# Weaving the high and low parts of three matmul operands in one SBUF tensor

## The reference

```python
# first block: four branches a, b, c, d, each of width 256
yi = y.reshape(B, S, BRANCH_W) * jax.nn.silu(z)
term = jax.nn.sigmoid(h @ w_merge[i]) * (yi @ w_br[i])
# second block, each of two layers
o = jnp.einsum('bhsm,bmhd->bshd', p.astype(v.dtype), v).reshape(B, S, D_MODEL)
x = x + o @ w_o                                        # memory output
x = x + (jax.nn.silu(h @ w_gate) * (h @ w_up)) @ w_down  # down projection
```

## Time and profile before

| | |
|---|---|
| median of 3 runs | 1111.04 us (1110.3 to 1111.07) |
| the profiled execution, span | 1111.3 us (no other time of it is recorded) |
| TensorE matmuls | 1092.0 us busy, 98%, 6251 instructions |
| TensorE weight loads | 951.6 us busy, 86%, 6251 instructions |
| VectorE | 749.5 us, 67% |
| ScalarE | 583.6 us, 53% |
| GpSimd | 54.4 us, 5% |
| HBM | 193 MB read, 175 GB/s over the span |

### The profile page before, as it was taken

The page is one execution under the profiler, slowest core; times in us unless marked ns, Lnnn a source line. Parts: engine busy times, 40 slices in busy tenths (PEclk is TensorE's granted clock), DMA queues, the critical chain, the costliest instruction groups (busy, mean ns, idle before and its releaser), DMA issues.

```text
span 1111.3 us, 15418 instructions
## 1 busy us (share of the span) xinstructions
PE 1092.0 (98%) x6251; PEld 951.6 (86%) x6251; DVE 749.5 (67%) x1024; ACT 583.6 (53%) x940; POOL 54.4 (5%) x87
## 2 busy tenths in 40 slices
PE   8999999999999999999999999999999999999997
PEld 6799988788898988989988988788988989888986
DVE  5736776865679977555678855546967546788643
ACT  3458653444477775555444544456765545444442
POOL 3311000000010000001000000000011000000000
PEclk9999999999999999999999999999999999999999
DMA  9956464655654325535555555544445435555550
GB/s 343 381 161 207 135 196 162 233 184 189 223 168 126 115 77 189 175 99 149 197 184 184 196 182 196 189 153 151 152 153 189 132 115 190 190 190 189 162 179 38
DMA packets 118776, 195.09 MB, mean 176 GB/s; under 512 B 6586, under 2 KB 39762, under 8 KB 118705
## 3 DMA queue, kind: packets, MB, share of 16 engines
q1 hardware_dynamic: 116144, 187.51, 50.7%
q0 software_dynamic: 2560, 6.60, 2.0%
HBM read 193.04 MB, written 1.05 MB: 175 GB/s over the span
## 4 chain that ended last, share of the span: by engine, by line
PE 83%; DVE 10%; ACT 5%; issue 1%; DMA 1%; POOL 1%; SPq 0%; DVEq 0%; ACTq 0%; POOLq 0%
PE product L669 55%; PE small L706 5%; PE product L706 5%; DVE conv_out L2719 5%; PE product L708 3%; PE small L708 3%; PE product L996 3%; ACT w_high L591 1%; ACT diagonal L2612 1%; DVE w_low L601 1%; PE small L816 1%; PE small L2081 1%; PE small L731 1%; PE small L1462 1%; PE small L1451 1%
## 5 line engine op out<-in xcount | busy, mean ns | idle before, releaser
L601 DVE TENSOR_TENSOR w_low<-w_raw,w_high 128x2048 fp32r<-128x2048 f32 (+3 forms) x160 | 350.0, 2190 | 180.2 <-ACT w_high L591 178.6
L591 ACT ACTIVATE w_high<-w_raw 128x2048 fp32r<-128x2048 f32 (+3 forms) x160 | 292.1, 1832 | 175.9 <-PE product L669 144.2
L669 PE MATMUL product<-w_high,H 128*128 128x512 f32 (+2 forms) x736 | 239.7, 393 | 0.5 <-DVE w_low L601 0.5
L669 PEld LDWEIGHTS product<-w_high,H 128*128 128x128 f32 x736 | 137.9, 188 | 26.9 <-DVE w_low L601 0.9
L669 PE MATMUL product<-H,w_high 128*128 128x256 f32 x816 | 150.9, 283 | 0.1
L669 PE MATMUL product<-w_low,H 128*128 128x512 f32 (+2 forms) x368 | 142.3, 387 | 0.0
L669 PEld LDWEIGHTS product<-H,w_high 128*128 128x128 f32 x816 | 126.6, 188 | 1.1 <-DVE w_low L601 0.5
L669 PE MATMUL product<-H,w_low 128*128 128x256 f32 x408 | 114.2, 280 | 0.0
L706 PE MATMUL product<-H,w_high 128*128 128x512 f32 x256 | 89.1, 391 | 0.0
L706 PE MATMUL small<-H,w_high 128*128 128x512 f32 x256 | 89.1, 391 | 0.0
L669 PEld LDWEIGHTS product<-w_low,H 128*128 128x128 f32 x368 | 69.3, 188 | 11.9 <-issue 0.2
(11 more groups left out here) (412 smaller groups left out, 1784.3 us busy)
## 6 DMA issues: line engine op xcount, KB each, us to landing
w_raw<-in_ffn_w_gate SPq DMA_DIRECT2D x20, 1024.0 KB, 5.0
w_raw<-in_ffn_w_up SPq DMA_DIRECT2D x20, 1024.0 KB, 5.0
w_raw<-in_ffn_w_down SPq DMA_DIRECT2D x20, 1024.0 KB, 5.0
w_raw<-in_w_merge SPq DMA_DIRECT2D x16, 1024.0 KB, 5.2
w_raw<-in_w_ada SPq DMA_DIRECT2D x32, 256.0 KB, 6.5
w_raw<-in_mem_w_k SPq DMA_DIRECT2D x8, 1024.0 KB, 5.0
w_raw<-in_mem_w_v SPq DMA_DIRECT2D x8, 1024.0 KB, 5.0
w_raw<-in_conv_w_pw SPq DMA_DIRECT2D x16, 512.0 KB, 4.7
```

The source lines that it names most:

```text
L591: k.act.eng.activation(parts_of(k, i, j)[0], raw_of(k, i), ACT.Copy).then_inc(*k.act.tells("weights_high", ("weights high", i)))
L601: k.vec.eng.tensor_tensor(low, raw, high.bitcast(F32), ALU.subtract).then_inc(*k.vec.tells("weights_low", ("weights low", i)))
L669: mm = pe.eng.matmul(bank[:, off:off + wide], a, r, start=b not in started, stop=True, skip_group_check=True)
```

## The change

A new method makes one tensor in which each element is followed by its partner: high, low, high, low. The two views step two elements, 8 bytes. Three operands get it in place of the pair. Sizes, the places of all other tensors, the instructions, their order and their waits stay the same.

```diff
+    def woven(self, name, tiles, n=S):
+
+        both = self.sb(name, [P, tiles, n, 2], F32R)
+        return both[:, :, :, 0], both[:, :, :, 1]
...
-        pairs = [self.pair(f"y_op{i}", BW // P) for i in range(2)]
+        pairs = [self.woven(f"y_op{i}", BW // P) for i in range(2)]
...
-        o = self.pair("o_mem", KT)
+        o = self.woven("o_mem", KT)
...
-        hidden = self.pair("hidden", FT)
+        hidden = self.woven("hidden", FT)
```

## The result

The changed kernel took 1118.35 us as the median of 4 runs (1116.63 to 1119.14), the kernel before 1111.05 (4 runs). The ratio is 1.0059, with a 95% interval of 1.0044 to 1.0075. Forecast was 1105.7.

What follows compares the result with a forecast made beforehand. TensorE's matmuls were taken to bound the kernel. Cheaper loads (-6.1 us) and VectorE's waits (+0.8) summed to -5.3 us, put on the median 1111.04: 1105.7 us, range 1101.5 to 1123.5.

Steps and rivals of the forecast that it cites:

- The bound: Whole kernel: TensorE's matmuls cover 98% of the span, so each nanosecond a down-projection matmul gains or loses reaches the total.
- The excess as the lever: Down projection: each matmul pays 13.7 ns over its 213.3 ns stream, which the stationary operand's layout can change.
- Streams in step: 816 matmuls: woven loads keep pace with the moving stream, so most excess goes, 7.5 ns each, -6.1 us; chance 46%.
- The 396-column row: Profile matmuls of 396 columns, 181.3 ns each, excess 16.3 ns; read as showing that the excess follows addresses.
- B: 816 stationary loads: woven loads fetch twice the bytes and the 13.7 ns excess doubles, +11.2 us, total 1123; chance 33%.
- a mild form of B: 816 woven loads no longer fit in one piece: 3 ns more each, +2.4 us, total 1114.2.
- The 104 ns of a load: Time of one stationary load by itself, from 64-column matmuls; gave a woven load's pace as 9.8 bytes/ns against the stream's 9.6.
- the 256-column row: Profile matmuls of 256 columns, 116.7 ns each, paced by the load, which takes some 12 ns longer beside a stream.
- Rival C: Stationary loads: their step doesn't matter and 16-byte lines need just two hits, so no change, 1111.8 us; chance 21%.
- VectorE's +0.8 us: Memory output: VectorE's stepped instructions take 0.2 us longer, four of them on the path; all others covered.
- the bound of 64: ScalarE's 34 stepped writes: at most 64 ns more for 512 elements, 2.2 us in all, hidden.
- The offsets: Moving weight chunks: offsets of 32 and 64 bytes, read as distances from a line, might let a load fit one piece.

Runs made afterwards that it cites:

- e1: Kernel before with only hidden woven (high and low parts alternating, step 8 bytes), memory and branch outputs left as pairs: 1115.48 us, ratio 1.0036.
- e11: Kernel before with hidden's two tensors 16 bytes behind the 256-byte line, unit step, nothing else changed: 1113.15 us, ratio 1.0028.
- e3: Kernel before, unit step, each tile of hidden and o_mem beginning 16 bytes further on: single tiles between 228.8 and 234.3 ns.
- e4: Hidden woven at 8 bytes, each tile 16 bytes further on, o_mem at a 16-byte step: hidden's tiles 231.1 to 234.8 ns, o_mem's matmuls 236.0 ns apart.
- e5: Kernel before, hidden as unit-step pairs, each weight chunk at its own place, 16 to 192 bytes behind the 256-byte line; no whole time given.
- e13: Unit step, both parts of the moving chunks 240 bytes behind the line, hidden at another place for each chunk: 1123.1 us.
- e8: Hidden laid out differently for each chunk: unit step, 8 or 16 bytes, woven or in separate tensors; a step of 8 bytes cost 6.5 ns, 16 bytes 8.2.
- e2: Changed kernel with hidden put back to a pair, only o_mem and y_op woven: 1112.74 us, ratio 1.0020.
- e12: Changed kernel with the woven hidden 48 bytes behind the line: 1114.13 us, ratio 1.0035 to the kernel before.

## Why the prediction was wrong

**The bound: right.** TensorE sets the time, and the nanoseconds of distance arrived in the whole: 4.4 us by the distances and 4.0 by the ratio in e1, 2.7 and 3.1 in e11.

**The excess as the lever: right.** It moved with the stationary operand's step and place, and no other wait grew.

**Streams in step: wrong. This is the step that failed.** "Two streams in step meet either never or at once ... Then most of the excess goes." The term of -6.1 us (816 x 7.5 gained) was +5.7 (hidden 528 x 8.3, o_mem 192 x 4.2, y_op 96 x 5.1 lost). Three errors lie under it. First, I took the pair's 13.7 ns for an average of random meetings, from which a regular pattern could only gain. It was already the lowest value: no layout in any run came under 226.6 for a whole chunk, and every other place tried at unit step gave 229.4 to 234.0 ns when held for a chunk with the moving operand on the line (226.6 only in e11's column 2). The 396-column row was the sign of this. Its 181.3 ns probably stood for what a mismatch costs; I used it only to show that addresses matter, and priced a lost match as a mild form of B at 3 ns. Second, the paces weren't equal as read. The 104 ns of a load are a mean with a short first distance in it: the eight starts of L1462 are 55 ns and then 110 to 112 ns apart, so a woven load goes at 1024/111 = 9.2 bytes/ns by the same reckoning, not 9.8, beside 9.6 for the stream; the 256-column row then pays some 5 ns over the load, not 12. Third, a mechanism that only equates two paces says nothing of the number of reads. Averaged over places, the slid pair of e3 has 231.7 ns, the slid woven operand of e4 232.7: in mean places weaving costs about 1 ns. Most of the rest is the good case at 226.7 that unit step can settle in and that weaving wasn't seen to reach at any of its thirteen places. Whether it can't, and how load and stream hold each other up, stays open; that they meet in banks, as the prediction supposed, no run shows.

**Rival B: right in sign, right for part of the size.** Doubling the excess would have been +13.7 ns; 8.3, 4.2 and 5.1 were measured, and its milder form (places no longer fit) named a part of it, priced at 3 ns. That reads were stolen in whole pieces was not shown; e5 and e11 refute it as the only cause.

**Rival C: wrong**, though its rule on two hits for a line nearly holds for the durations at 8 bytes: VectorE 0, ScalarE 46 and the load's record 8 ns more.

**VectorE's +0.8 us: wrong, 0.** 690 ns before and after; half of the bound from a row with 1024-byte hops was too much. The Trainium skill's rule that a port keeps its rate only for adjacent pairs of words (Vector Engine (DVE) Microarchitecture Reference, 5.2 Measured stream behaviour on trn2) doesn't hold at a step of 8 bytes here: 692 ns at 4 and 8 bytes, 1095 at 16. **ScalarE: right**, 46 ns more for 512 elements of hidden and 34 for o_mem, under the bound of 64, hidden.

**The offsets** were misread: an offset in a buffer was taken for a distance from the line, without the buffer's own start. It didn't enter the sum, but read rightly it would have shown both operands on a line and made it worth asking what another place costs.

**The range** reached to 1123.5 and holds 1118.35; the chance of slower was put at 0.35.

## What to carry to other kernels

An fp32r matmul of 512 columns pays 13.4 to 23 ns over its stream here, and how much depends on the step of the stationary operand, on the places of both operands and on what ran before; the distance between starts shows it and the busy time doesn't. Before changing a layout to lower such a price, put the present operand at a few other places (one run with another place for each chunk shows six): if all are worse, the layout is probably in its best case already, and a change that moves it is likely to lose. Look at each repetition by itself before taking a mean: two means here hid two cases each. Keep a stationary fp32r operand at unit step, and check addresses with the start of the buffer, not the offset alone.

## What the runs showed of the hardware

- Distance between starts of 512-column fp32r matmuls with 128-column loads, full clock: 226.7 ns at best (544 cycles of 2.4 GHz for 512 columns), mostly 229 to 236 at unit step in other places of either operand, 230.3 to 235.8 at 8 bytes, 234.9 to 236 at 16. At the lower clock it is 426.7 ns, the stream alone (e4).
- With one layout the distance can have two steady values: 233.3 and 226.6 ns (e11, hidden 16 bytes behind the line), 235.6 and 233.3 (the changed kernel), 226.7 and 236.4 (e13, chunk 2).
- The Trainium skill (SBUF — State Buffer, Who interferes with whom) says that TensorE's two read ports are independent and that TensorE never waits on anyone. No run shows the ports, but where the load reads isn't free for TensorE: moving the stationary operand by 16 bytes, with nothing else changed, costs 3.1 us (e11).
- Step and duration: the load's record is 187 to 193, 192 to 201 and (median) 314 ns at 4, 8 and 16 bytes; VectorE's 512 elements 692, 692 and 1095 ns; ScalarE's, from SBUF, 633, 679 and about 1140 (e8; the extreme of the row below, from min/median/max ns).

```profile
L2329 ACT ACTIVATE hidden<-mid x14: 631/683/1141, 537.8 to 1047.5; 128x512 fp32r<-128x512 f32 x14
```

- Near 190 us the granted clock is at its lower level for 3.4 or 6.8 us in some executions and not in others (not in the profiled ones of e1, e2, e11 and e12); in e4 it falls instead at the start of both memory outputs, near 486 and 899 us, after TensorE had stood idle for 1.8 us. Near 190 us TensorE runs two rounds of eight matmuls of 8 columns before the fall, and the same two in e11, where the clock doesn't fall; what decides is not shown. It adds 1.7 or 3.4 us, as much as some of the effects measured here; a small effect is to be read from distances between starts, not from two times.
